# Routed experts in chunks of 32 slots: four experts side by side on TensorE, a second set of first matrices copied over by GpSimd

## The reference, cut to what matters

```python
gate = jax.nn.one_hot(g_sel[:, 0], N_GROUPS, dtype=jnp.float32)[:, :, None] * exp_w[:, None, :]
out = jnp.zeros_like(t)
for gi in range(N_GROUPS):
    hid = jax.nn.silu(jnp.einsum('td,edf->tef', t, w1[gi])) * jnp.einsum('td,edf->tef', t, w3[gi])
    hid = hid * gate[:, gi, :, None].astype(hid.dtype)
    out = out + jnp.einsum('tef,efd->td', hid, w2[gi])
```

## Time and profile before

| | |
|---|---|
| median of 3 runs | 1279.66 us (1276.83 to 1282.75) |
| the profiled execution | 1282.53 us, its span 1280.7 us |
| busy share of the span | PE 95%, weight loads 77%, DVE 58%, ACT 41%, GpSimd 4% |
| mean granted TensorE clock | 0.971 of full speed |
| HBM read | 281.87 MB, 222 GB/s over the span |
| expert loop | 1013.8 to 1263.1 us |
| after the loop's last matmul | 17.6 us to the end of the span |

### The profile page before, as it was taken

The page is one execution under the profiler, slowest core; times in us unless marked ns, Lnnn a source line. Parts: engine busy times, 40 slices in busy tenths (PEclk is TensorE's granted clock), DMA queues, the critical chain, the costliest instruction groups (busy, mean ns, idle before and its releaser), DMA issues. The chain is left out here.

```text
span 1280.7 us, 18685 instructions
## 1 busy us (share of the span) xinstructions
PE 1212.9 (95%) x7413; PEld 989.2 (77%) x7413; DVE 743.4 (58%) x1239; ACT 520.4 (41%) x892; POOL 54.1 (4%) x94
## 2 busy tenths in 40 slices
PE   7898999999899999999999999999998899999995
PEld 5887799999699879999888677888876666666663
DVE  3577778777766677777875245564557622222224
ACT  4567434443455544343362322455432222222222
POOL 5000000000000000000000000000000000000000
PEclk9999999999999999999989878999999899999998
DMA  9942377788553338887642411644456399999960
GB/s 274 270 165 96 120 273 276 277 277 292 165 198 122 110 120 313 291 289 277 245 113 58 143 66 67 202 165 164 165 223 236 136 386 405 405 405 404 404 274 33
DMA packets 124549, 285.04 MB, mean 223 GB/s; under 512 B 11549, under 2 KB 72218, under 8 KB 115904
## 3 DMA queue, kind: packets, MB, share of 16 engines
q1 hardware_dynamic: 114416, 248.76, 54.2%
q0 software_dynamic: 10064, 35.32, 8.4%
HBM read 281.87 MB, written 2.20 MB: 222 GB/s over the span
## 5 line engine op out<-in xcount | busy, mean ns | idle before, releaser
L1794 DVE TENSOR_TENSOR w_lo<-ring,w_hi 128x1024 fp32r<-128x1024 f32 (+1 forms) x272 | 319.5, 1211 | 94.7 <-ACT w_hi L1354 85.9
L1354 ACT ACTIVATE w_hi<-ring 128x1024 fp32r<-128x1024 f32 (+1 forms) x272 | 277.5, 1050 | 149.8 <-PE acc L601 131.2
L599 PE MATMUL pp<-x_hi,w_hi 128*128 128x256 f32 x896 | 260.5, 291 | 5.6 <-DVE w_lo L1794 3.5
L600 PE MATMUL pp<-x_lo,w_hi 128*128 128x256 f32 x896 | 256.6, 286 | 0.0
L601 PE MATMUL pp<-x_hi,w_lo 128*128 128x256 f32 x896 | 256.4, 286 | 0.0
L599 PEld LDWEIGHTS pp<-x_hi,w_hi 128*128 128x128 f32 x896 | 174.8, 195 | 14.5 <-issue 9.5
L600 PEld LDWEIGHTS pp<-x_lo,w_hi 128*128 128x128 f32 x896 | 175.0, 195 | 1.4 <-issue 0.2
L601 PEld LDWEIGHTS pp<-x_hi,w_lo 128*128 128x128 f32 x896 | 174.9, 195 | 0.0
L599 PE MATMUL acc<-w_hi,x_hi 128*128 128x512 f32 (+2 forms) x320 | 127.6, 399 | 5.3 <-DVE x_lo L1779 4.2
L601 PE MATMUL acc<-w_hi,x_lo 128*128 128x512 f32 (+2 forms) x320 | 123.5, 386 | 0.0
L600 PE MATMUL acc<-w_lo,x_hi 128*128 128x512 f32 (+2 forms) x320 | 123.2, 385 | 0.0
(11 more groups left out here) (359 smaller groups left out, 1867.3 us busy)
## 6 DMA issues: line engine op xcount, KB each, us to landing
ring<-in_w_up_dram SPq DMA_DIRECT2D x32, 1024.0 KB, 5.3
ring<-in_w_down_dram SPq DMA_DIRECT2D x32, 1024.0 KB, 6.8
ring<-in_w_dram SPq DMA_DIRECT2D x32, 1024.0 KB, 9.6
stage<-in_w_ada_dram POOLq DMA_DIRECT2D x48, 512.0 KB, 6.4
ring<-in_w_in_dram SPq DMA_DIRECT2D x24, 1024.0 KB, 5.0
big<-in_w_dram SPq DMA_DIRECT2D x24, 1024.0 KB, 8.4
ring<-in_w_in_a_dram SPq DMA_DIRECT2D x12, 1024.0 KB, 14.8
ring<-in_w_kv_shared_dram SPq DMA_DIRECT2D x8, 1024.0 KB, 6.2
```

The costliest lines, as they stand in the source:

```text
L599: pe.matmul(out, lhs[0], rhs[0], start=start, stop=False)
L600: pe.matmul(out, lhs[0], rhs[1], start=False, stop=False)
L1354: act.activation(shaped(high_half(b, k), raw), raw, ACT.Copy).then_inc(S["hi_ready"], 1)
L1794: dve.tensor_tensor(shaped(low_half(b, k), raw), raw, shaped(high_half(b, k), raw), ALU.subtract).then_inc(S["lo_ready"], 1)
```

## The change

A chunk is four experts (a quad) with 32 slots each. A quad takes as many chunks as its own fullest expert needs, where before the fullest of all experts set the rounds of all. DVE works out the chunks' table (`tabs`: where each quad's chunks end, and the quad of each chunk); every engine runs `Fori(0, chunks)` and reads the quad from the table. In a chunk the four experts lie side by side on TensorE, 32 columns of the array each, for w1, w3 and w2. Gathering is done once in float32 (`u_tm`) in place of twice on split parts, and the split (L2328, L2329) is gone; DVE writes `u_tm` with a stride.

There are 16 slots of 1 MB in place of 12: `w3_slots` and `w2_slots`, four each, and `w1_slots`, eight. They lie over `ring`, `w_hi` and `w_lo`. TensorE reads w1 from slots 0 to 3 alone. SP loads the next quad's w1 into slots 4 to 7, and GpSimd copies it over to slots 0 to 3, in four copies of 128x2048, when the quad before has used its own for the last time. SP's order for each quad s is w3(s), w2(s), w1(s+1), four DMAs of 1 MB each. They wait for the last use of w3(s-1), for that of w2(s-1), and for GpSimd's copy of w1(s).

```diff
-SLOTS = 64
+SLOTS = 32
 ROUNDS = SEQ // SLOTS
-STEPS = EXPERTS // 4
+QUADS = EXPERTS // 4
+CHUNKS = ROUNDS * QUADS
...
+        with nc.sbuf_tensor("exp_ring", [128, 8, 2048], f32) as exp_ring:
+            w1_slots = exp_ring
...
-        e_ring = [v_tm[:, :, :].rearrange("p a b -> p (a b)"), stage[:, :, :].rearrange("p a b -> p (a b)"),
-                  mod[:, 0:2048], big[:, 0:2048], big[:, 2048:4096], big[:, 4096:6144]]
-        e_ring += [ring[:, slot_of(B_WO + i), :] for i in range(4)]
-        e_ring += [o_tm[:, :, :].rearrange("p a b -> p (a b)"), q_t[:, :, :].rearrange("p a b -> p (a b)")]
-        plan = carve(1, ROUNDS * STEPS + 1, 16)
+        w3_slots = [stage[:, :, :].rearrange("p a b -> p (a b)"), mod[:, 0:2048], big[:, 0:2048], big[:, 2048:4096]]
+        w2_slots = [big[:, 4096:6144], v_tm[:, :, :].rearrange("p a b -> p (a b)"), mod[:, 2048:4096],
+                    o_tm[:, :, :].rearrange("p a b -> p (a b)")]
...
+            def load_w1(s, e):
+                load_part(w1_slots[:, (4 if s else 0) + e, :], w1[4 * s + e, :, :, :], S["w1_here" if s else "w1_full"])
+
+            def load_w3(s, e):
+                load_part(w3_slots[e], w3[4 * s + e, :, :, :], S["w3_full"])
+
+            def load_w2(s, e):
+                load_part(w2_slots[e], w2[4 * s + e, :, :, :], S["w2_full"])
...
+            for i in range(4):
+                sp.wait_ge(S["lo_ready"], half_index(B_WO + i, 1) + 1)
+                load_w1(0, slot_of(B_WO + i))
+            sp.wait_ge(S["half_used"], half_index(B_WO + 3, 1) + 1)
+            load_w2(0, 1)
+            for e in range(4):
+                load_w1(1, e)
+            sp.wait_ge(S["r_out"], 3)
+            load_w2(0, 2)
+            load_w2(0, 3)
...
+            for s in range(1, QUADS):
+                done = sp.value_load(tabs[0:1, s - 1:s], min_val=1, max_val=CHUNKS)
+                sp.wait_ge(S["w3_used"], done)
+                for e in range(4):
+                    load_w3(s, e)
+                sp.wait_ge(S["w2_used"], done)
+                for e in range(4):
+                    load_w2(s, e)
+                if s + 1 < QUADS:
+                    sp.wait_ge(S["w1_moved"], 4 * s + 1)
+                    for e in range(4):
+                        load_w1(s + 1, e)
...
+            pool.wait_ge(S["trips_ready"], 1)
+            for s in range(1, QUADS):
+                done = pool.value_load(tabs[0:1, s - 1:s], min_val=1, max_val=CHUNKS)
+                pool.wait_ge(S["w1_here"], 64 * s)
+                pool.wait_ge(S["w1_used"], done)
+                for e in range(4):
+                    pool.tensor_copy(w1_slots[:, e, :], w1_slots[:, 4 + e, :]).then_inc(S["w1_moved"], 1)
...
-            def gather(g):
-
-                for c in range(2):
-                    f = slice(256 * g + 128 * c, 256 * g + 128 * c + 128)
-                    out = gather_bank[g][:, 256 * c:256 * c + 256]
+            def gather(half):
+
+                for j in range(4):
+                    f = slice(512 * half + 128 * j, 512 * half + 128 * j + 128)
                     for q in range(QT):
-                        pe.matmul(out, u_hi[:, q, f], sel[:, q, :], start=(q == 0), stop=False)
-                        last = pe.matmul(out, u_lo[:, q, f], sel[:, q, :], start=False, stop=(q == 1))
+                        last = pe.matmul(y_bank[half][:, 128 * j:128 * j + 128], u_tm[:, q, f], sel[:, q, :],
+                                         start=(q == 0), stop=(q == 1))
                 last.then_inc(S["xe_ready"], 1)
...
+            def up(part, weight):
+
+                for kt in range(KT):
+                    for e in range(4):
+                        last = pe.matmul(up_bank[32 * e:32 * e + 32, 256 * part:256 * part + 256],
+                                         xe[:, kt, 32 * e:32 * e + 32], weight(e, slice(256 * kt, 256 * kt + 256)),
+                                         start=(kt == 0), stop=(kt == KT - 1))
+                return last
+
+            with pe.Fori(0, chunks) as i:
+                quad = pe.value_load(tabs[0:1, bass.ds(i + 8, 1)], min_val=0, max_val=QUADS - 1)
+                pe.wait_ge(S["w1_full"], 64)
+                pe.wait_ge(S["w1_moved"], quad * 4 + 1)
+                pe.wait_ge(S["xe_done"], i * 2 + 2)
+                up(0, lambda e, cols: w1_slots[:, e, cols]).then_inc(S["w1_used"], 1)
+                pe.wait_ge(S["w3_full"], quad * 64 + 64)
+                up(1, lambda e, cols: w3_slots[e][:, cols]).then_inc(S["w3_used"], 1)
+
+                pe.wait_ge(S["sel_ready"], i + 2)
+                pe.wait_ge(S["y0_low"], i + 1)
+                gather(0)
+                combine(0)
+                pe.wait_ge(S["y1_low"], i + 1)
+                combine(1)
+
+                pe.wait_ge(S["gsel_ready"], i + 1)
+                pe.wait_ge(S["hid_done"], i + 1)
+                for f in range(2):
+                    pe.transpose(turn_bank[:, 128 * f:128 * f + 128], hid_e[:, 128 * f:128 * f + 128], ident)
+                for q in range(QT):
+                    last = pe.transpose(turn_bank[:, 256 + 128 * q:384 + 128 * q], gsel[:, q, :], ident)
+                last.then_inc(S["turn_ready"], 1)
+                gather(1)
+
+                pe.wait_ge(S["w2_full"], quad * 64 + 64)
+                pe.wait_ge(S["turned_done"], i + 2)
+                for half in range(2):
+                    pe.wait_ge(S["xe_done"], i * 2 + 3 + half)
                     for f in range(2):
-                        pe.transpose(turn_bank[:, 128 * f:128 * f + 128], hid_e[:, 128 * f:128 * f + 128], ident)
-                    for q in range(QT):
-                        last = pe.transpose(turn_bank[:, 256 + 128 * q:384 + 128 * q], gsel[:, pair, q, :], ident)
-                    last.then_inc(S["turn_ready"], 1)
-                    if pair == 1:
-                        gather(2)
-
-                    pe.wait_ge(S["turned_done"], i * 2 + (pair + 2))
-                    for half in range(2):
-                        if pair == 1:
-                            pe.wait_ge(S["xe_done"], i * 4 + (6 + half))
-                        for f in range(2):
-                            for e in range(2):
-                                o = 6 * pair + 4 + e
-                                if half == 0 and f == 0:
-                                    pe.wait_ge(e_full[o], i * 16 + 16)
-                                last = pe.matmul(y_bank[half][64 * e:64 * e + 64, :],
-                                                 turned[:, 128 * f + 64 * e:128 * f + 64 * e + 64],
-                                                 e_ring[o][:, 1024 * f + 512 * half:1024 * f + 512 * half + 512],
-                                                 start=(f == 0), stop=(f == 1))
-                        if half == 0:
-                            last.then_inc(S["y0_ready"], 1)
-                            if pair == 1:
-                                gather(3)
-                        else:
-                            last.then_inc(S["e_used"], 2)
-            pe.wait_ge(S["y0_low"], steps * 2 + 1)
+                        for e in range(4):
+                            last = pe.matmul(y_bank[half][32 * e:32 * e + 32, :],
+                                             turned[:, 128 * f + 32 * e:128 * f + 32 * e + 32],
+                                             w2_slots[e][:, 1024 * f + 512 * half:1024 * f + 512 * half + 512],
+                                             start=(f == 0), stop=(f == 1))
+                    last.then_inc(S["y0_ready" if half == 0 else "w2_used"], 1)
...
-                dve.tensor_tensor(o_tm[:, q, :], o_tm[:, q, :], mod[:, 3072:4096], ALU.add).then_inc(S["r_out"], 1)
+                by_row, by_tile = "p (j k) -> p j k", "p (k j) -> p j k"
+                dve.tensor_tensor(u_tm[:, q, :].rearrange(by_tile, k=KT), o_tm[:, q, :].rearrange(by_row, k=KT),
+                                  mod[:, 3072:4096].rearrange(by_row, k=KT), ALU.add).then_inc(S["r_out"], 1)
...
-                u, hi, lo = o_tm[:, q, :].rearrange("p (j k) -> p k j", k=KT), by_tile(u_hi, q), by_tile(u_lo, q)
-                link(dve.tensor_copy(hi, u))
-                dve.tensor_tensor(lo, u, hi, ALU.subtract).then_inc(S["u_split"], 1)
...
+                dve.tensor_tensor(by_slot(sel), iota[:, 0:SLOTS].unsqueeze(1).to_broadcast([128, 8, SLOTS]),
+                                  now[:, :].unsqueeze(2).to_broadcast([128, 8, SLOTS]), ALU.is_equal)\
+                    .then_inc(S["sel_ready"], 1)
...
+                quad = dve.value_load(tabs[0:1, bass.ds(i + 9, 1)], min_val=0, max_val=QUADS - 1)
+                dve.wait_ge(S["sel_ready"], i + 1)
+                dve.tensor_tensor(by_slot(gsel), by_slot(sel), gate_now[:, :].unsqueeze(2).to_broadcast([128, 8, SLOTS]),
+                                  ALU.mult).then_inc(S["gsel_ready"], 1)
                 dve.wait_ge(S["gsel_ready"], i + 1)
```

(40 more changed lines are left out.)

210 lines of the change are left out of this document (73 added, 137 removed).

## The result

The changed kernel takes 1259.46 us (median of 4 runs, 1254.31 to 1261.31) where the kernel before took 1278.88 (4 runs, 1276.83 to 1282.75). The ratio is 0.983, with a 95% interval of 0.981 to 0.985. The prediction was 1256, with 1247 to 1280 as its range. The profiled execution of after took 1258.51 us, its span 1256.7 us, at a mean granted clock of 0.951.

The account below looks back on a forecast made before the run. The prediction took the loop to be bound by TensorE, with loads only just covered. A schedule of loads, copies and ten chunks ended the loop 23.3 us earlier, which from the median 1279.66 gives 1256 us, range 1247 to 1280.

Parts of the forecast that it names:

- TensorE's chunk: Expert loop on TensorE: four matmuls run together in 0.43 us a group, so a chunk takes 16.8 us.
- The first two rivals: TensorE's groups of four take 0.86 us, not together (chance 0.12), or 0.54 us, partly together, giving 1271 us (chance 0.1).
- the first rival: Four matmuls do not run together on TensorE: 0.86 us a group, 27 us a chunk, 1313 us in all; chance 0.12.
- How many chunks: Expert loop: quads 1 and 3 take two chunks, the rest one; 10 chunks, 168 us of TensorE in place of 249.
- GpSimd's copies: Copying w1 between slots: 2.2 us a copy, bounds 1.9 to 6.0, four copies 8.8 us.
- The third rival: GpSimd's w1 copies take 4.2 us or more each: 1278 us at 4.2, 1313 at 6.0; chance 0.1.
- Loads: Weight loads in the expert loop: 10.0 us for four matrices, plus 2 us from the last byte to the semaphore.
- The clock: TensorE restarts at half rate after new pauses before single-chunk quads; 2.3 to 5.3 us lost, 2.3 taken.
- The fourth rival: TensorE's pauses cost nothing and GpSimd's copies are quick: down to 1246 us; chance 0.06.
- The start: Ahead of the first chunk: cheaper `select` and gathering, strided `u_tm` costing 0.5 us; start at 1012.9 in place of 1013.8.
- What was said to show it: Profile signs: 10 chunks, 28 copies at 2.2 us, SP waiting only around quads 1 and 3, 18.5 us after the last copy.
- The sum: Schedule of the whole loop: last chunk ends at 1239.8 against 1263.1, 23.3 us less, giving 1256.4 us.

Follow-up runs that it names:

- the kernel with the pairs kept apart: The changed kernel with a chunk's experts multiplied two at a time and a 128x128 transpose between the pairs in each product; 1306.48 us, ratio 1.019 to the kernel before.
- the first experiment: The changed kernel with the four experts of a chunk multiplied two at a time, still in 32-column tiles; 1284.46 us, ratio 1.004 to the kernel before.

## Why the prediction was right, point by point

The mechanism, the chunks and TensorE's waits were as forecast; the sum was 3.1 us short (1256.4 against 1259.46), made of small terms of both signs. As a saving, 23.3 us were forecast and 19.4 came. Times from the loop's start, 1012.9 in the forecast and 1009.51 in after:

| | forecast | after | of that |
|---|---|---|---|
| w3 of quad 0 used up | +7.4 | +7.1 | |
| w3 of quad 1 used up | +40.9 | +41.8 | TensorE waited for w2(1) |
| w1(3) landed | +72.9 | +75.5 | restart of the loads +1.6 |
| w1(3) copied | +81.7 | +82.9 | copies -1.4 |
| w3 of quad 3 used up | +107.6 | +109.5 | clock +0.7 |
| w1(5) landed | +139.6 | +143.1 | restart +1.6 |
| w1(7) landed | +199.6 | +203.4 | rate +0.3 |
| w1(7) copied | +208.4 | +210.8 | copies -1.4 |
| last w2 product done | +226.9 | +229.6 | |

**TensorE's chunk**: right in the group's length, 0.43 us. That the chunk came out so near, 16.5 us against 16.8, is in part luck: in after its pieces (6.91, 3.77, 1.85, 0.44 and 3.57 us) fill the 16.54 us, so gathering took 3.8 us, not 3.5, and the 0.6 us for entering the loop were not there. The first two rivals, that four tiles run together not at all or in part, fall with it: their groups would have been 0.86 and 0.54 us. The forecast could only argue from spare room in issuing; now rows show it, and in the kernel with the pairs kept apart, if not everywhere, the time was 47 us longer, some 6 us of it the added transposes. The schedule that priced the first rival (a chunk of 27 us, 1313) was sound: it gives, within 2 us, the times measured with chunks of 20.9 and 24.2 us.

**How many chunks**: right, 10, and the rest of the schedule stood on it.

**GpSimd's copies**: at the low end of the bounds. From GpSimd's timeline in after:

```profile
1152.61 7.40 POOL L573 COPY exp_ring<-exp_ring 128x2048 f32<-128x2048 f32 x4 [29.53 <-DMA exp_ring<-in_w_dram]
1182.74 7.40 POOL L573 COPY exp_ring<-exp_ring 128x2048 f32<-128x2048 f32 x4 [22.74 <-DMA exp_ring<-in_w_dram]
1212.87 7.40 POOL L573 COPY exp_ring<-exp_ring 128x2048 f32<-128x2048 f32 x4 [22.72 <-DMA exp_ring<-in_w_dram]
```

All 28 took 1.89 us, where 1.9 to 6.0 were the bounds. The third rival, 4.2 us or more, falls; why L539 in the earlier trace rows was slow was not tried. Taking 2.2 us put 2 x 1.4 us too much on the path, the one term that erred upward by more than a microsecond.

**Loads: the step that failed.** The rate was right: the rows just shown are 30.13 us apart, 10.04 us for four matrices. What was mis-sized is what a pause of the queue costs. Against the 2 us behind the last byte, taken from the 192 KB transfer of the earlier trace rows, stood no time ahead of the first. From the release of w3 to the landing of w1 there were forecast 32.0 us and came 34.0 (1016.6 to 1050.6), 33.6 (1051.3 to 1085.0) and 33.6 (1119.0 to 1152.6). The windows of after show where:

```profile
1051.00:1052.00 1.00, 1.00 (x14) 0.74 (x7) 0.19 (x1) 0.38 (x1) 1.00 (x1) 1.00 0.00 0
1052.00:1053.00 1.00, 1.00 (x11) 1.00 (x11) 0.23 (x1) 0.00 (x0) 1.00 (x2) 1.00 0.97 131
1053.00:1054.00 1.00, 1.00 (x7) 0.87 (x7) 0.00 (x0) 0.60 (x1) 1.00 (x1) 1.00 0.79 319
1054.00:1055.00 1.00, 1.00 (x7) 0.74 (x6) 0.00 (x0) 0.00 (x0) 1.00 (x2) 1.00 0.98 418
```

The first load is issued at 1051.38; in the 2.6 us to 1054 the queue moves (131 + 319) / 418 = 1.1 us' worth, so some 1.5 us are gone before it runs full. Three restarts cost 1.6 to 2.0 us each more than forecast. What is left of the 33.6 us beside the 30.1 of a full queue and this start, 2.0 us, is the landing, as forecast. The row of the 192 KB transfer was one number for both ends, and the forecast put all of it at one.

**The clock**: right in kind, in size partly by luck. After a pause TensorE began at 0.50 (from 1092 to 1098 us before quad 3; 0.55 over the first 5 us of the last chunk), and the product pair took 9.92 and 9.13 us in place of 6.91 before quads 3 and 7: 3.0 and 2.2 us lost, forecast 2.3 each. In the second profile of after the same two took 8.89 and 10.01, so 2.0 to 3.1 us are lost a pause. The forecast's 2.3 came from a misread row: in the earlier trace rows the window from 50 to 52 us, in which TensorE restarts at 50.8, stands at 0.99, so the low clock lasted from about 52 to 55.4 us and cost 1.7 us. The fourth rival, pauses that cost nothing, falls. Its other half, quick copies, was right. The cost of the pauses was not tried by itself; it is read from these rows.

**The start**: the sign was right, the size was not. 0.9 us were to be gained before the first product. From the second tile's modulation (L2310, 987.61 before; L2319, 983.49 after) to the first product it is 26.21 and 26.02 us: 0.2 gained. The strided writing of `u_tm` took 1.90 us a tile where L2312 took 1.30 or less: 1.2 us in all against 0.5.

**What was said to show it.** SP's waits were to appear only around quads 1 and 3. They stand in all seven turns, as shown above; it was the DMA engines that stood only there and, as forecast, before the loop's first release of w3 (3 GB/s from 1010 to 1015). The forecast took a queue's wait and idle DMA for the same thing, which changed no number. From the last copy to the last w2 product it took 18.8 us, forecast 18.5.

**The sum.** In the loop the restarts add 0.9 (the first, in part hidden), 1.6 and 1.6 us, the clock 0.7, the rate 0.3 and the last chunk 0.3, and the copies take off 2.8: 2.6 us too long, with 2.7 read. With the start's 0.7 that is 3.4 us, against 3.1 in the medians. Two entries of the forecast are 0.6 us less than its own terms, which it does not explain: from the copied w1(3) to w3 of quad 3 used up it counts 25.9 us where 16.8 + 7.4 + 2.3 are 26.5, and for the last chunk 18.5 where 16.8 + 2.3 are 19.1. Measured were 26.6 and 18.8. Written out, its terms give 1257.6.

## What to carry to other kernels

When a kernel is near two bounds at once, price a change that eases one of them as a schedule of the other: cutting TensorE's work from eight steps of 31 us to ten chunks of 17 brought 3.6 us of loop with twelve slots and 19.7 with sixteen. A queue that is made to stand has a price at both ends, here 1.5 us before it runs full and 2.0 us from the last byte to the semaphore. And before copies are made faster or dropped, look at what order the loads come in: a different order gave 6 to 7 us, dropping nearly all of the copying gave 2.

## What the runs showed of the hardware that was not expected

**Tiles of TensorE run ahead of each other.** A matmul on free columns starts before those on other columns that stand ahead of it in the program: eight records behind, 0.02 us later, in the first experiment. Over the products with w1 and w3 this saved 2.5 of 13.8 us. A transpose over all columns between them ended it. The Trainium skill ("TensorEngine Tiling (Array Packing)", Key Properties) says that tiles operate independently and can load and multiply in parallel; the trace agrees, the first expectation had not reckoned with it. How far ahead TensorE looks was not tried.

**DVE is held up by GpSimd's copies.** While a group of copies ran (1050.61 to 1058.02), the making of `hid_hi` took 1.75 us:

```profile
1056.41 1.75 DVE L2463 TENSOR_SCALAR hid_hi<-scr 128x256 fp32r<-128x256 f32 x1 [4.19 <-ACT scr L1723]
```

It has one SBUF input and takes 0.29 us in the loop's other chunks, by the median of ten. Its neighbours with two SBUF inputs met no copy here. It was not on the path, so it cost nothing. The other kernels bear it out. Without copies (twelve slots), and with copies of 128 columns, all ten took 0.29 us. With the copies doubled, five of the ten began within a copy and took 1.01 to 1.71 us, and each ended 0.14 us after that copy did; the first of them, and its copy:

```profile
1024.86 1.26 DVE L2464 TENSOR_SCALAR hid_hi<-scr 128x256 fp32r<-128x256 f32 x1 [4.19 <-ACT scr L1724]
...
1024.08 1.90 POOL L573 COPY exp_ring<-exp_ring 128x2048 f32<-128x2048 f32 x1
```

In that kernel `gsel`, `now` and `sel` met copies too and took up to 1.72, 1.84 and 2.08 us, where they take 0.43, 0.15 and 0.42 alone: the hold-up that the prediction reckoned with for them. The Trainium skill ("SBUF — State Buffer", two separate sides) has a VectorE instruction in a mode that uses the shared port pair excluded by a GpSimd instruction for its whole length; the trace agrees, since in after too `hid_hi` ends 0.14 us after the copy in which it began.
